# Two-part tiles: contraction steps of the next projection tile ahead of a compressed turn, the first local scores and the second unit's turn

## The reference, cut to what matters

```
def masked_softmax(s, mask): ...
s_cmp = jnp.einsum('bghsd,bgnd->bghsn', q, kc)
p_cmp = masked_softmax(s_cmp, cmp_mask)
o_cmp = jnp.einsum('bghsn,bgnd->bghsd', p_cmp.astype(vc.dtype), vc)
...
o = gt[..., 0:1] * o_cmp + gt[..., 1:2] * o_slc + gt[..., 2:3] * o_win
...
return o * norm_g * jax.nn.silu(og)          # gla_mixer
```

## Time and profile before

| what | value |
|---|---|
| median of 3 runs | 1380.76 us |
| the profiled execution, its own time | 1381.55 us |
| span of that execution | 1379.7 us |
| PE busy | 1353.6 us (98%) |
| DVE busy | 1035.9 us (75%) |
| ACT busy | 879.9 us (64%) |
| POOL busy | 493.1 us (36%) |
| HBM read | 231.57 MB, 169 GB/s over the span |

### The profile page before, as it was taken

How to read it: one execution, slowest core, us unless ns; L and a number is a source line. 1 busy time by engine, 2 the same in 40 slices (tenths; PEclk the granted TensorE clock), 3 DMA queues, 4 the chain that set the end, 5 groups by cost and what they waited for, 6 DMA issues and landing times.

```text
span 1379.7 us, 31435 instructions
## 1 busy us (share of the span) xinstructions
PE 1353.6 (98%) x13296; PEld 1160.9 (84%) x13296; DVE 1035.9 (75%) x1463; ACT 879.9 (64%) x1442; POOL 493.1 (36%) x402
## 2 busy tenths in 40 slices
PE   9999999999999999999999999999999999999997
PEld 7778888888788888888778888889888778988887
DVE  5897975569898854568887988756978866898853
ACT  5686765347676863446895755555787888675652
POOL 0143760124146830225210566503114211366610
PEclk9999999999999999999999999999999999999999
DMA  9543566544443656525336465552643334375551
GB/s 367 186 143 134 176 224 212 190 158 155 140 150 138 237 195 213 190 100 170 123 114 223 145 220 186 170 193 93 224 144 123 108 123 146 131 252 207 199 168 32
DMA packets 37020, 234.64 MB, mean 170 GB/s; under 512 B 4752, under 2 KB 7824, under 8 KB 10384
## 3 DMA queue, kind: packets, MB, share of 16 engines
q1 hardware_dynamic: 36880, 232.63, 49.0%
HBM read 231.57 MB, written 1.05 MB: 169 GB/s over the span
## 4 chain that ended last, share of the span: by engine, by line
PE 75%; DVE 14%; ACT 6%; issue 2%; POOL 1%; DMA 1%; ACTq 0%; SPq 0%; DVEq 0%; POOLq 0%
PE psum L744 22%; PE psum L746 21%; PE psum L745 21%; DVE low L2511 5%; PE psum L848 1%; PE psum L850 1%; PE psum L849 1%; PE psum L969 1%; ACT high L1768 1%; ACT m L2219 1%; PE psum L973 1%; DMA raw<-stream 1%; POOL h L3412 1%; POOL m L3410 1%; DVE arena L2666 1%
## 5 line engine op out<-in xcount | busy, mean ns | idle before, releaser
L2511 DVE SCALAR_TENSOR_TENSOR low<-raw,high 128x2048 f16<-128x2048 f32 (+5 forms) x247 | 518.3, 2105 | 180.4 <-ACT high L1768 179.7
L744 PE MATMUL psum<-u,high 128*128 128x256 f16 (+2 forms) x1924 | 529.8, 275 | 2.2 <-ACT arena L1754 1.4
L746 PE MATMUL psum<-u,low 128*128 128x256 f16 (+2 forms) x1924 | 529.5, 275 | 0.0
L745 PE MATMUL psum<-u,high 128*128 128x256 f16 (+2 forms) x1924 | 529.5, 275 | 0.0
L1768 ACT ACTIVATE high<-raw 128x2048 f16<-128x2048 f32 (+4 forms) x248 | 418.3, 1690 | 120.4 <-PE psum L746 88.6
L744 PE MATMUL psum<-arena,high 128*128 128x256 f16 (+3 forms) x1208 | 331.0, 274 | 1.8 <-DVE arena L3109 1.4
L746 PE MATMUL psum<-arena,low 128*128 128x256 f16 (+3 forms) x1208 | 330.9, 274 | 0.0
L745 PE MATMUL psum<-arena,high 128*128 128x256 f16 (+3 forms) x1208 | 330.9, 274 | 0.0
L744 PEld LDWEIGHTS psum<-u,high 128*128 128x128 f16 x1924 | 188.1, 98 | 34.4 <-issue 4.9
L745 PEld LDWEIGHTS psum<-u,high 128*128 128x128 f16 x1924 | 188.3, 98 | 27.9 <-issue 0.7
L746 PEld LDWEIGHTS psum<-u,low 128*128 128x128 f16 x1924 | 188.2, 98 | 27.4
(11 more groups left out here) (381 smaller groups left out, 1904.9 us busy)
## 6 DMA issues: line engine op xcount, KB each, us to landing
raw<-stream SPq DMA_DIRECT2D x206, 1024.0 KB, 4.8
raw<-stream SPq DMA_DIRECT2D x8, 768.0 KB, 4.3
raw<-stream SPq DMA_DIRECT2D x5, 512.0 KB, 3.9
raw<-stream SPq DMA_DIRECT2D x2, 896.0 KB, 4.5
con<-consts SPq DMA_DIRECT2D x1, 1437.0 KB, 12.3
h<-x_t SPq DMA_DIRECT2D x2, 512.0 KB, 5.7
raw<-stream SPq DMA_DIRECT2D x2, 448.0 KB, 5.2
misc<-small SPq DMA_DIRECT2D x1, 512.0 KB, 14.4
```

The costliest lines, as they stand in the source:

```text
L744: pe.matmul(out, w_hi, x[0], start=start, stop=False)
L745: pe.matmul(out, w_hi, x[1], start=False, stop=False)
L746: return pe.matmul(out, w_lo, x[0], start=False, stop=stop)
L2511: tell(dve.scalar_tensor_tensor(low[:, at:at + w], raw[:, off:off + w], W_SCALE, high[:, at:at + w], ALU.mult, ALU.subtract), split_ready ...
```

## The change

`tile_in_parts` does contraction steps `ks` of a tile: the waits of `single_tile` stand before step 0, and `tile_done` is counted after step 7. It is used at three places. In each first-kind layer, steps 0 and 1 of tile T_OG + 2 move from behind `pooled_out` to ahead of `compressed_turn(0)`. In the griffin layer, steps 0 to 2 of tile GQ[4] move ahead of `scores(0)`, and steps 0 to 3 of tile GG[1] move ahead of `turn(1)` and `scores(3)`. On ACT, `evac(T_OG + 1)` moves from behind `copy_pt(4)` into the middle of `exps(5)`, between its second and third exp.

```diff
+            def tile_in_parts(name, j, rhs, n, ks):
+
+                step = next(step for step in products[name]["steps"] if j in step[1])
+                if ks[0] == 0:
+                    await_slot(step[0])
+                    bank_free(products[name]["first"] + j)
+                for k in ks:
+                    mm = tile(name, step, k, j, rhs, n)
+                if ks[-1] == KT - 1:
+                    mm.then_inc(tile_done, 1)
@@ PE, first_layer
                 turn(4)
                 one(T_OG + 1)
+                tile_in_parts(f"in1_{l}", IN1_NTH[T_OG + 2], x_at, S, range(0, 2))
                 compressed_turn(0)
                 values(4)
                 compressed_turn(1)
                 turn(5)
                 pooled_out()
-                one(T_OG + 2)
+                tile_in_parts(f"in1_{l}", IN1_NTH[T_OG + 2], x_at, S, range(2, KT))
                 compressed_out()
                 values(5)
@@ PE, griffin
                 one(GQ[3])
+                tile_in_parts("in_g", GQ[4], x_at, T, range(0, 3))
                 scores(0)
-                one(GQ[4])
+                tile_in_parts("in_g", GQ[4], x_at, T, range(3, KT))
@@
                 scores(2)
                 values(0)
+                tile_in_parts("in_g", GG[1], x_at, T, range(0, 4))
                 turn(1)
                 scores(3)
-                one(GG[1])
+                tile_in_parts("in_g", GG[1], x_at, T, range(4, KT))
                 values(1)
@@ ACT, first_layer
-                def exps(p):
+                def exps(p, between=None):
@@
                     for g in range(2):
                         for b in range(2):
                             n = 2 * g + b
                             ins = act.activation(e_pair[q][:, g, b, 0:nk], ...)
+                        if between and g == 0:
+                            between()
                     tell(ins, attn_exp)
@@
                 copy_out(3)
-                exps(5)
+                exps(5, lambda: evac(T_OG + 1))
                 copy_pt(4)
-                evac(T_OG + 1)
                 copy_ptc(0)
```

## The result

The changed kernel takes 1390.55 us (median of 6 runs, 1389.99 to 1391.94); the kernel before, run again beside it, 1381.11 us (6 runs, 1380.73 to 1381.49). The ratio is 1.007, 95% interval 1.0057 to 1.0083: slower, by more than the noise. The time lies 2.65 us above the forecast of 1387.9 and 0.55 us above the upper end of the range. In the layers the hold that the forecast names happened, and the low clock of rival D came on top of it; griffin gave less than reckoned.

What follows compares the result with a forecast made beforehand. PE was taken as the bound, busy 1353.6 of 1379.7 us. The profiled 1381.55 plus 7.8 for the layers' hold less 0.67 for griffin gave 1388.7, less 0.79 to the median 1387.9 us; 8-of-10 range 1380.3 to 1390.

Steps and rivals of the forecast that it cites:

- the hold that the forecast names: First-kind layers: the second gate operation on DVE starts behind POOL's long one and is held, 3.9 us per layer.
- rival D: Out1 in both layers: as forecast, but the clock falls behind the stalls, 2.0 us more per layer, 1391.9 us; chance 0.08.
- step k = 0: Out1 in the first-kind layers: PE takes this step 3.9 us later, behind the delayed low part, 7.8 us for both layers.
- PE's side of the layers: At compressed_turn(0): the moved steps take 0.65 us of work for 0.33 of delay, winning 0.33 us per layer.
- change of weights from a full to a narrow tile: Ahead of compressed_turn(0): going from full to narrow weights costs 0.20 us from start to start.
- the margin at the gate: First-kind layers: the second gate operation starts 0.12 us behind POOL's long one; before, it started 0.02 us ahead.
- two anchors: The held gate's end, reckoned from POOL's start (106.02) or the end of the DVE operation under way (105.70); 105.87 taken.
- Rival C: Second gate operation: held as long as POOL's whole operation, 5.9 us per layer, 1391.9 us; chance 0.04.
- Griffin: Griffin layer: the units' chain on ACT, DVE and POOL ends 0.67 us earlier, with bounds 0 and 1.3.
- `scores(0)`: Griffin layer: three steps of GQ[4] ahead of it win 0.72 us, and it starts 0.32 us late.
- The 4.2 us of PE's waits: Four waits at the places of the change, in both layers and griffin, taken as the most the idea can reach.
- Rival A: First-kind layers: the hold misses the second gate operation; layers lose 0.8, griffin gives 0.67, 1380.9 us, no change; chance 0.27.

Runs made afterwards that it cites:

- experiments 2: The changed kernel with both griffin splits undone, so only the first-kind layers' part stays: 1390.51 us, ratio 1.0071 to the kernel before.
- experiment 3: The changed kernel with all PE splits undone; only ACT's evac(T_OG + 1) inside exps(5) stays: 1390.78 us, ratio 1.0071 to the kernel before.
- experiment 6: The changed kernel plus 32 idle matmuls ahead of out1 in both first-kind layers: 1387.99 us, ratio 1.0049 to the kernel before.
- experiments 1: The changed kernel with the layers' splits and the exps(5) move undone, so griffin's splits alone: 1381.18 us, ratio 0.9999 to the kernel before.
- 4: The changed kernel, with POOL's long operation also waiting for the second gla_mixed: 1382.15 us, ratio 1.0008 to the kernel before.
- Experiment 5: The changed kernel plus 5 idle matmuls ahead of pooled_out in both first-kind layers: 1381.78 us, ratio 1.0004 to the kernel before.
- 10: Of the whole change only griffin's GQ[4] split, one run: 1380.83 us, against 1380.86 to 1381.89 for the kernel before.
- 11: Of the whole change only griffin's GG[1] split, one run: 1381.44 us, against 1380.86 to 1381.89 for the kernel before.
- experiment 7: The changed kernel with POOL's long operation cut into four pieces: 1382.45 us, ratio 1.0009 to the kernel before.

## Why the prediction was right, and where it was wrong

The cause that the forecast names, the second gate operation held behind POOL's long one, is what the runs show. The step that failed is the one on where PE waits: the prediction set the whole delay at step k = 0 and left out that out1's first tile needs bank 0. The runs showed one wait of 3.41 us for that bank instead, and behind it the low clock, to which the prediction had given a chance of 0.08.

- **PE's side of the layers.** Forecast 0.33 us per layer, measured 0.47 in the first. The term that was most off is the change of weights from a full to a narrow tile: 96.24 to 96.35, 0.11 and not 0.20. So POOL came earlier than I reckoned and the margin at the gate was 0.27 us, not 0.12; it made the hold surer and changed nothing else.
- **The hold by the order of the starts.** Right, in both layers. In the ten kernels that have the long operation in one piece, in both layers, the gate operation took 3.75 where it started 0.27 to 0.44 us behind POOL (after; experiments 2 and 3; 6, with POOL at 100.79 and the gate at 101.07) and 0.42 to 0.43 where it started first (before; 1, with 101.11 and 101.09; 4, 5, 10 and 11). Experiment 5 adds 0.55 us of idle PE work per layer, nothing else, and turns it over.
- **Its length.** Forecast an end at 105.87, which is 105.39 on the time axis of after; measured 105.24. The prediction took the middle between two anchors, and the rows decide for the second, the end of the DVE operation under way (105.70, which is 105.22 here). In all ten kernels, in both layers, POOL's operation started while a DVE operation was under way; that one ran on unhindered, and the next one ended 3.78 us behind its end (in after 101.04 + 0.42 = 101.46 and 101.49 + 3.75 = 105.24; in experiment 3 101.84 and 105.62; before 101.91 and 105.68, to the rounding). From POOL's start the same end lies 3.94 to 4.19 behind. POOL's own record goes on for 1.45 us more each time, here to 106.70, so its length too (5.40 to 5.64) follows the DVE operation under way. Rival C, the hold for POOL's whole operation (the Trainium skill, "SBUF — State Buffer", "SBUF: two separate sides"), would have ended at 106.70 + 0.42 = 107.12, 1.88 us later: what that section says of who contends and that the first to start keeps the port agrees with the rows; "for the whole instruction" does not.
- **Where PE waits.** This step failed. I spread the delay over new waits up to step k = 0 and set its size there. But out1's first tile goes to bank 0, which T_OG + 2 holds, and its evacuation stands in the very list of delayed ACT operations that the prediction gives. The wait is one piece of 3.41 us at the first matmul. For the size alone this is worth little: in experiment 6, where the clock stays up, k = 0 is taken at 112.50. The gate operation starts there 0.42 us earlier than in after (101.07 and 101.49), and after's time axis lies 0.48 ahead of before's, so this is 113.40 on the axis of before, 3.58 us behind the 109.82 of the earlier trace rows; the forecast was 3.9. (Its upper bound of 4.12 per layer should have been 4.08 by its own terms, which changes nothing.)
- **The clock.** Because the wait is one piece, rival D came on top of the forecast. I had given it a chance of 0.08 and 2.0 us per layer; it took 1.29 and 1.61 us of slow matmuls (13 and 16 of them 0.21 us apart), of which 0.55 per layer would have been lost around k = 0 anyway, as experiment 6 shows there. That leaves 1.8 us for both layers in these two traces, and the medians of after and 6 are 2.6 apart. It decided against the range: without it the kernel takes 1387.99 us. That this is 0.1 from the forecast is partly luck: the layers cost 7.2 there and not 7.8, and griffin gave 0.15 and not 0.67.
- **Griffin.** Forecast 0.67 us, measured 0.15 at out_g (0.18 in experiments 1 and 10). The step that failed is `scores(0)`: it comes 0.83 us late, not 0.32. GQ[4] is the first tile of a slot of its own, and its low part was not ready when GQ[3] ended. After: PE, then DVE:

```profile
659.40 0.29 PE L744 MATMUL psum<-u,high 128*128 128x272 f16 x1 [0.33 <-DVE low L2526]
...
660.55 1.16 PE L1472 MATMUL psum<-arena 64*128 64x128 f32 x16
```
```profile
657.06 2.28 DVE L2526 SCALAR_TENSOR_TENSOR low<-raw,high 128x2048 f16<-128x2048 f32 x1
```

  The low part ends at 659.34 and PE starts at 659.40. The prediction looked at the bank and at the weights' slot only where they come free, never at where GQ[4]'s slot is filled. The rest held: GG[1]'s gain came back as a wait at `values(1)`, and out_g waits 1.44 us as before.
- **Profiled execution and median.** The sum was made against the profiled execution, 1388.7, which measured 1390.12: 1.43 us off, by the layers (9.00 against 7.8) and griffin (0.15 against 0.67), less 0.29 elsewhere (mostly the 0.48 of the start). Another 1.2 of the 2.65 between forecast and median is the step from one to the other: I took 0.79 off, but the execution profiled before lay 0.44 above the median of the six runs, and the one of after 0.43 below, with the short slow parts described above.
- **Why no version gains.** The 4.2 us of PE's waits could not be had. 1.66 of them stood in griffin, whose chain PE doesn't set. In the layers the evacuation that frees bank 0 delays DVE's gates (0.47 forecast, 0.49 measured: 101.04 + 0.48 against 101.03), and PE's step k = 0 had 0.09 us of slack for it: even with the hold turned away (4, 5, 7) the time is 1381.8 to 1382.5. Rival A had 1380.9 for this case.

## What to carry to other kernels

When an edit shifts two engines by different amounts, line up their starts against each other at every later place where a long POOL operation meets DVE work, and not only along the waits: an order held by 0.02 us, which no semaphore fixes, was worth 8 to 9 us here, and one wait on POOL fixed it. Follow a delayed engine's whole list down to the first operation that frees a bank or a slot; the wait falls there, and a wait like this one of 3.4 us costs more than its length: here PE came back at 1.2 GHz, for 1.3 us or more per layer. Before a piece of a tile is pulled ahead, look at when its weights are ready, not just its bank.

## What the runs showed of the hardware

- A DVE operation that starts 0.27 to 0.44 us behind a POOL operation of 5.5 us took 3.75 us instead of 0.42 (after; experiments 2, 3 and 6). What is constant in all ten kernels is the distance from the DVE operation that was under way when POOL started: the held one ended 3.78 us behind its end, and 1.45 us ahead of POOL's recorded end (105.24 and 106.70 in the first layer of after). What releases it the runs don't tell; spans on POOL are rough.
- With POOL's work in four operations of 1.5 to 1.7 us, the same DVE operation took 0.71 (experiment 7).
- In the first layer of after, a PE wait of 3.41 us was followed by a granted clock of 0.54 in the next 3 us and 1.00 in the 3 us after; in the second layer, behind the same wait, it was 0.62 from 408 to 411 us. How many matmuls ran slowly behind such a wait differed between executions, from 13 to 27. 32 idle matmuls in the wait kept the clock at 1.00 (experiment 6).
- The weights' change from `split_matmul` to `compressed_turn` cost no more than an ordinary start (0.11 in after, 96.24 to 96.35), while the way from there to `values` cost 0.20 before (97.40 to 97.60).
